# Gathered rows dotted earlier, three weight tiles asked for earlier, last sums token tile by token tile (hybrid encoder block, PEER stage)

## What is computed

```python
def _peer(x, wq, subkeys, u, v):              # x: 512 x 1024 ; u, v: 16384 x 1024
    q = (x @ wq).reshape(n, 8, 2, 128)        # 8 heads, two halves
    s = einsum('nhpd,hpkd->nhpk', q, subkeys)  # top 16 of 128 for each half
    cand = s_top[:, :, 0, :, None] + s_top[:, :, 1, None, :]
    best_s, best_j = top_k(cand, 16)          # 16 experts a head: 128 picks a token
    gate = softmax(best_s)
    h = einsum('nd,nhkd->nhk', x, u[expert])
    coef = gate * gelu(h)
    return einsum('nhk,nhkd->nd', coef, v[expert])
h = layernorm(alpha * h + peer(h), ln2_g, ln2_b)
```

## Time and profile before

| | |
|---|---|
| runs | 2085.87, 2084.53, 2076.84 us; median 2084.53 |
| profiled execution | 2081.93 us, its span 2080.2 us |
| mean granted TensorE clock | 0.957 |
| busy share | PE 92%, DVE 74%, ACT 37%, POOL 28% |
| traffic | 416.5 MB, mean 200 GB/s |

### The profile page before, as it was taken

One profiled execution on the slowest core, in us unless ns is written; L12 is line 12 of the kernel. 1 busy time (PEld: TensorE's weight loads), 2 busy tenths in 40 slices (PEclk: granted clock), 3 DMA queues, 4 the chain that ended last, 5 costly groups with the idle time before them and its releaser, 6 DMA issues.

```text
span 2080.2 us, 34092 instructions
## 1 busy us (share of the span) xinstructions
PE 1909.4 (92%) x13250; PEld 1617.5 (78%) x13250; DVE 1537.8 (74%) x2826; ACT 761.0 (37%) x1113; POOL 581.0 (28%) x403
## 2 busy tenths in 40 slices
PE   5989998789999879999999999969999999999892
PEld 4968876348974359999999999958888788888782
DVE  6277993314545269999978888748877788799998
ACT  3222554532210033333446666523333333332320
POOL 2322343000000035555531011222222222266661
PEclk9988998897999999999999999989999999999997
DMA  3211232010023034344567777899999999999994
GB/s 124 71 61 47 86 111 71 0 42 3 4 79 126 0 146 138 131 132 134 172 234 277 267 272 267 307 322 361 339 364 344 345 346 349 312 356 389 382 347 152
DMA packets 173719, 416.53 MB, mean 200 GB/s; under 512 B 13952, under 2 KB 89216, under 8 KB 170384
## 3 DMA queue, kind: packets, MB, share of 16 engines
q1 hardware_dynamic: 119728, 256.16, 36.0%
q0 software_dynamic: 36864, 134.23, 17.2%
q10 hardware_dynamic: 16992, 24.26, 3.2%
HBM read 363.08 MB, written 51.51 MB: 199 GB/s over the span
## 4 chain that ended last, share of the span: by engine, by line
PE 34%; DVE 24%; DMA 4%; issue 2%; SPq 0%; ACT 0%; DVEq 0%; ACTq 0%
PE ps L2006 18%; PE ps L1921 8%; DVE h_tok L1561 7%; PE ps L1925 4%; PE ps L1979 3%; DVE w_hl L2144 2%; DVE is_place L2088 2%; DVE is_place L2083 1%; DVE picks L2091 1%; DVE top_at L2049 1%; DVE top_at L2058 1%; DVE s_head L2052 1%; DMA coef<-parked_gelu 1%; DMA gates<-dense_gates 1%; DMA h1T<-in_v 1%
## 5 line engine op out<-in xcount | busy, mean ns | idle before, releaser
L2006 PE MATMUL ps<-w_hl,coef_hl 128*128 128x512 f32 x2304 | 539.1, 394 | 28.3 <-DVE coef_hl L2174 28.3
L2006 PEld LDWEIGHTS ps<-w_hl,coef_hl 128*128 128x128 f32 x2304 | 432.9, 189 | 130.5 <-DVE coef_hl L2174 37.0
L1921 PE MATMUL ps<-h_hl,w_hl 128*128 128x384 f32 (+1 forms) x2304 | 446.6, 345 | 19.9 <-ACT h1T L1826 11.1
L1921 PEld LDWEIGHTS ps<-h_hl,w_hl 128*128 128x128 f32 x2304 | 406.4, 189 | 33.2 <-ACT w_hl L1855 11.4
L1542 POOL DMA_INDIRECT gathered_rows<-in_u_rows,pick_index x128 | 137.5, 1074 | 538.2 <-DVE pick_hidden L1552 529.2
L1925 PE MATMUL ps<-h_hl,w_hl 128*128 128x384 f32 (+1 forms) x1152 | 230.0, 340 | 0.0
L1855 ACT ACTIVATE w_hl<-w_staged 128x1024 fp32r<-128x1024 f32 x143 | 152.0, 1063 | 188.9 <-PE ps L2006 137.2
L1925 PEld LDWEIGHTS ps<-h_hl,w_hl 128*128 128x128 f32 x1152 | 203.4, 188 | 5.0
L1542 POOL DMA_INDIRECT gathered_rows<-in_v,pick_index x128 | 164.8, 1288 | 148.4 <-DVE h_tok L1561 97.9
L1795 POOL TENSOR_TENSOR w_hl<-w_staged,w_hl 128x1024 fp32r<-128x1024 f32 x64 | 163.7, 2561 | 135.5 <-ACT w_hl L1820 111.1
L1561 DVE SCALAR_TENSOR_TENSOR h_tok<-gathered_rows,pick_hidden,h_tok 128x1024 f32<-128x1024 f32 x128 | 164.1, 1282 | 10.0 <-DVE h_tok L1561 0.5
(11 more groups left out here) (315 smaller groups left out, 2546.8 us busy)
## 6 DMA issues: line engine op xcount, KB each, us to landing
w_staged<-in_stream SPq DMA_DIRECT2D x132, 512.0 KB
h1T<-in_v SPq DMA_DIRECT2D x66, 512.0 KB
w_staged<-in_v SPq DMA_DIRECT2D x62, 512.0 KB
dense_gates<-lot SPq DMA_DIRECT2D x24, 1024.0 KB
gates<-dense_gates SPq DMA_DIRECT2D x16, 1536.0 KB
w_staged<-in_w_in_t SPq DMA_DIRECT2D x40, 512.0 KB
parked_gelu<-h1T ACTq DMA_DIRECT2D x102, 192.0 KB
coef<-parked_gelu SPq DMA_DIRECT2D x102, 192.0 KB
```

The source lines that it names most:

```text
L1921: nc.tensor.matmul(ps[:, bank, 0:width], w_hl[:, j % RING, 0, P * k:P * (k + 1)], h_hl[:, part, k, lo:SEQ], start=(k == 0 and part == 0), ...
L2006: last = nc.tensor.matmul(ps[:, 2 + 2 * t + half, :], coef_hl[:, k % HLS, c, P * t:P * (t + 1)], w_hl[:, s % RING, v, 512 * half:512 * (ha ...
```

## The change

Dots: two a lot instead of one, three a tile behind instead of two (48 + 18 = 66 by k = 0). In the parked stage 1.1 a tile (178 by k = 101), so `DOTTED` is k = 56. The 78 adds that are left are spread over k = 102 to 124, and the last three k have none. Loads: the v tiles of k = 0, 1, 2 are asked for ahead of the loads of lot 22. Sums: after hidden(127), the sums of the last three k go token tile by token tile, and DVE's tail waits for its own token tile alone.

```diff
     BEHIND = PARKED - (4 * PEER_HEADS + BETWEEN + 2 * LOTS)
-    used_behind = [LOTS + 2 * (n + 1) for n in range(BEHIND)]
+    DOTS_A_LOT, DOTS_BEHIND = 2, 3
+    used_behind = [DOTS_A_LOT * LOTS + DOTS_BEHIND * (n + 1) for n in range(BEHIND)]
     EARLY = used_behind[-1]
-    used_by = [EARLY + (k + 1 if k < PARKED else PARKED + (2 * PICKS - EARLY - PARKED) * (k + 1 - PARKED) // FRESH)
+    A_PARKED = 1.1
+    BEFORE_FRESH = EARLY + int(A_PARKED * PARKED)
+    used_by = [EARLY + int(A_PARKED * (k + 1)) if k < PARKED else
+               min(2 * PICKS, BEFORE_FRESH + -(-(2 * PICKS - BEFORE_FRESH) * (k + 1 - PARKED) // (FRESH - HLS)))
                for k in range(EXPERT_KEYS)]
...
             for n in range(LOTS):
+                if n == LOTS - 2:
+
+                    load_from(QUERIES + PARKED, QUERIES + PARKED + 3)
                 first = FIRST_LOT + TILES_A_LOT * n + RING
                 load_from(first, min(first + TILES_A_LOT, QUERIES + PARKED))
...
             for k in range(COEFS):
                 load_parked(k)

-            load_from(QUERIES + PARKED, QUERIES + PARKED + 3)
             for j in range(2):
                 sp.wait_ge(act_parked[j], 16 * (PARKED // 2 + 1))
...
-            def sums(k):
+            def sums(k, tiles=range(TILES_D)):
...
-                for t in range(TILES_D):
+                for t in tiles:
...
-            for k in range(EXPERT_KEYS):
+            for k in range(EXPERT_KEYS - HLS):
                 if k + LEAD in U_AT:
                     hidden(k + LEAD)
                 sums(k)
+
+            hidden(EXPERT_KEYS - 1)
+            for t in range(TILES_D):
+                for k in range(EXPERT_KEYS - HLS, EXPERT_KEYS):
+                    sums(k, [t])
...
-                dot_rows(nc, dve, h_tok, gathering, n)
+                for x in range(DOTS_A_LOT * n, DOTS_A_LOT * (n + 1)):
+                    dot_rows(nc, dve, h_tok, gathering, x)
             for n in range(BEHIND):
                 low(FIRST_BEHIND + n + 1)
-                for x in range(used_behind[n] - 2, used_behind[n]):
+                for x in range(used_behind[n] - DOTS_BEHIND, used_behind[n]):
                     dot_rows(nc, dve, h_tok, gathering, x)
...
                 if t:
-                    dve.wait_ge(sum_done, EXPERT_KEYS)
+                    dve.wait_ge(sum_done, EXPERT_KEYS - HLS + HLS * t)
```

## The result

The changed kernel takes 2055.81 us (median of 4 runs, 2051.98 to 2070.54) against 2083.34 us before: ratio 0.9882, 95% interval 0.9835 to 0.9928. A second set of runs of the same kernel gave 2048.8 us, 0.9836 (0.9811 to 0.9861). So it is faster by 27 to 33 us. The forecast was 42.5 us and 2042.0; the direction and the range hold, the size is 9 to 15 us too large.

A forecast was written before the change was run, and what follows sets the result against it. PE was taken to bound the lots and parked stage, DVE the fresh stage alone. Terms of -38.5, -7 and +3 us gave -42.5 us: 2037.7 as profiled span, 2042.0 as median, range 2029 to 2058.

The forecast's parts named there:

- Fresh stage and tail: From hidden(102) to the end: PE bound at 8.30 us a step, DVE setting the tail's pace; -38.5 us, from -20 to -40.
- The wait for ln2's rows: In the tail: DVE waits for rows asked for just before hidden(127) ends; between 0 and 2 us, taken as 1.2.
- Lots: In the lots: 24 more dots fit DVE's waits for PE and the DMA has room; cost 0, bound 3 us.
- Entry: From lots into the parked stage: of 18 us idle time a gain of 3 to 14 us, taken as -7.
- the stop for the first v tile: Ahead of the last parked tile: PE's stop of 11.1 us goes with v tiles issued some 40 us earlier.
- DVE's third dot: Behind the lots: three dots and a low part take DVE 4.7 us a tile against PE's 4.2; sums(0) at 1366 to 1370.
- Of my rivals the second: Into the parked stage: early v tiles only hand PE's stop over to later waits, gain 0; 2049 us, chance 0.15.
- Parked stage: Parked tiles: ten more blocks delay 11 gates loads by 0.3 us each; +3 us, bounds 0 and 15.
- Rival 3: In the parked stage: DMA is full and every added byte is paid, 15 us instead of 3; 2054 us, chance 0.14.
- The room of 0.9 MB a period: In the parked stage: DMA has about 0.9 MB spare per eight tiles, of which the change takes 0.42 MB.
- Rivals 4 (fresh stage): In the fresh stage: PE takes 8.8 us a tile instead of 8.30, 13 us more; 2055 us, chance 0.11.
- 5 (slower by the clock): In the parked stage: each gates load stops PE and lowers its clock, 5 us a load; 2094 us, chance 0.04.

The follow-up runs named there:

- e3: The kernel before with the moved dots and adds alone, its last sums and loads the old ones: 2068.02 us, ratio 0.9926.
- e4: The kernel before with only the last three tiles' sums going token tile by token tile: 2080.98 us, ratio 1.0011.
- e2: The changed kernel with the first three v tiles at their old place, behind the gates and first coefficients: 2054.15 us, ratio 0.9869.
- e12: e8 with the v tiles at their old place, behind the first coefficients: 2040.28 us, ratio 0.9795.
- e8: The changed kernel with one dot a tile behind the lots instead of three and gates asked for four tiles earlier: 2042.39 us, ratio 0.9812.
- e6: The changed kernel with one dot a tile behind the lots instead of three: 2043.08 us, ratio 0.9810.
- e5: The kernel before with only the first three v tiles asked for ahead of lot 22's loads: 2079.69 us, ratio 0.9991.
- e10: e8 with 1.2 dots or adds a parked tile instead of 1.1: 2041.76 us, ratio 0.9807.
- e7: The changed kernel with the parked stage's gates asked for four tiles earlier: 2047.36 us, ratio 0.9823.
- e9: The changed kernel with 1.0 dot or add a parked tile instead of 1.1: 2050.52 us, ratio 0.9831.
- e11: e8 with the first three v tiles asked for behind the last parked tiles, ahead of the first gates: 2034.28 us, ratio 0.9762.

## Why the prediction was right or wrong

**Fresh stage and tail: right.** Forecast 211.7 us to the end of hidden(127) and 39.7 us less with the tail. Measured: hidden(127) ends 211.5 us behind the start of hidden(102) (1826.54 to 2038.06), the first tail operation is 4.5 us behind that, and stage and tail are 242.5 instead of 281.9 us, 39.4 less. The wait for ln2's rows, set at 1.2 us, didn't come: they were asked for 0.3 us ahead of hidden(127)'s end but landed in 4.2 and 5.1 us. e3 and e4 part the sum: 31 us are the moved adds, 8.2 the order of the last sums, which alone gives nothing.

**Lots: right in the dots, 0.** 265.2 us with two dots a lot (e2) and with one. The 0.7 us of the changed kernel are the early v tiles, put at 0 to 2.

**Entry: wrong, and this is the step that failed.** The term was -7 us, for 18 us of idle time that the prediction took from a window up to 1405.5, a few tiles behind sums(0). Its fair counterpart is therefore the time to tile 10, which grew by 4.0 us in both executions (the entry alone by 8.8). The step had three things wrong. First, it took the stop for the first v tile as a wait that an earlier place in the order would remove. The stop went, and 14.55 us for the first coefficients came: idle time ahead of sums(10) was 18.5 us before and 20.9 after. Second, it put the delay behind the early v tiles at nothing. Against e2 they pushed the last lot's store back by 5.4 us and the gates by 6, and the coefficients stand behind those. Third, it let DVE's third dot be next in line, with its gathers as something that only "competes" with the moved bytes. DVE is busy 27.64 of the 49.2 us; what its three dots a tile do is let POOL issue 18 gathers in the entry instead of 10, and the first coefficient load then took 24.9 us to issue instead of 10.2. With v tiles late, the time to tile 10 is 87.2 us at one dot a tile behind the lots (e12) and 97.6 and 98.4 at three (e3, e2); with them early it is 87.0 and 86.6 at one (e8, e6) and 93.3 at three. So the extra gathers lengthen it, and this is shown. That it is bytes over a rate is not: the entry is 49.1 to 49.2 us both at 339 GB/s (e2, share 0.94) and at 390 (the changed kernel, share 1.03). Of my rivals the second comes nearest (the early tiles only hand the stop over), and e5 shows the handing over on the kernel before: 11.1 us for the tile became 11.7 for the coefficients. But it put the outcome at 0, and nothing on my list had the third dot make the stage longer. I had the row for it: each gather brings 0.5 MB, and the best slice of the DMA was 407 GB/s.

**Parked stage: mechanism right, size low.** The forecast was +3 us through later gates, bounds 0 to 15; the ninety tiles, free of the entry's stops, measured +12.6 and +9.7. That is nearly as large an error as the entry's. DVE's waits for gates rose from 13.5 to 24.5 us, inside the 20 to 30 foreseen, but PE's idle time to 9.0 and 6.5 us, over the 3 to 5 foreseen. The 14.0 and 11.1 us lost in the ninety tiles are 5 us more than that idle time, in part through the half clock behind two of the stops in each execution, and the term of 0.3 us a load had no price for it. Rival 3, the full DMA, is refuted by e10. Gates asked for earlier leave no PE stop behind tile 10, with 1.1 and with 1.2 blocks a tile (e7, e8, e10); ten blocks fewer do nearly the same (e9, 372.3). The room of 0.9 MB a period does not follow from the two slices of the earlier trace rows: their difference, 138 GB/s over 4.12 us, is 0.57 MB a slice, 1.1 for two.

**Sum.** The stages before and after differ by 0.7 (lots) + 4.0 (to tile 10) + 12.6 (ninety) - 39.4 = -22.1 us in the first profile and by -25.1 in the second, against the forecast's -42.5. Of the 20 us between forecast and first profile the entry is 11, the parked stage 10 and the lots 0.7, and the fresh stage and tail give 0.9 back. The medians say -27 and -33; the stage lengths come from one execution each, and why the medians give more isn't settled: executions differ in the unchanged part, and only one of each kernel was profiled. Rivals 4 (fresh stage) and 5 (slower by the clock) did not happen, though the half clock behind a stop did, at two of the gates loads in each execution. That the result still fell in the range is owed to its width: by stages the change gave little more than half of the forecast.

## What to carry to other kernels

Work moved off a busy engine brings its transfers along, so price them at the new place. Where loads were already late, a block of 0.5 MB cost 0.56 us here with the v tiles early and some 0.9 with them late, not 0. Measure such a cost up to a point where all stalls of the stretch are over: up to the first sums it looked like 1.06 us, and part of that came back a few tiles later. A stall that names one late load among many isn't cured by asking for that load ahead of all others; it moved to the next load. Fewer bytes, or an order in which they come as they are needed (e11), did shorten the stretch. And check the pace of an engine that is shown busy throughout: two executions lost 7.2 us in a stage with no wait to show for it. Where a double buffer is free long before its refill is asked for, ask at once: four tiles earlier made a DMA share of 1.04 harmless.

## What the hardware showed that I had not expected

- A DMA share of 0.99 to 1.04 with TensorE hardly or never waiting: 349 GB/s before, 376 GB/s in e10. The share alone doesn't tell a full DMA from one with room.
- Issuing itself can take long: four loads of 192 KB kept SP for 26.70 us, 24.9 of them the first alone, and everything behind them in its order.
- After a stop of 4.6 us TensorE's granted clock was 0.65 and 0.52 in the next two slices of 4.12 us and 1.00 again in the third; of its two levels (1.2 and 2.4 GHz) that is the lower one for 6.8 us in all.
- The same matmuls of 512 columns ran at 229 ns each or, in whole stretches of e7 and e11, at 233, at a granted clock of 1.00 both times. The cause is open.
